# Expert weights fetched two slots at a time, and two narrow projections turned round, in a two-block model of one core

## The reference

```python
# block 1: one wide projection; 16 of its columns are the decay and beta inputs of the gated delta rule
(na_q, na_k, na_v, dn_qkv, dn_a, dn_b, dn_gate, df_q, df_k, df_v, ft_u) = split_proj(h_lat @ w_in)
g = -exp(a_log) * softplus(dn_a + dt_bias); beta = sigmoid(dn_b)
...
# block 1: 16 experts of width 2048, each takes the 32 tokens that score it highest
hid = silu(xg @ w_gate) * (xg @ w_up)
y = (hid @ w_down) * gate
```

## Time and profile before

| | |
|---|---|
| runs | 2237.03, 2241.74, 2240.36 us; median 2240.36 us |
| the profiled execution | 2242.1 us, of which the profile's span is 2240.3 us |
| PE busy | 1891.1 us (84%), 11984 instructions |
| DVE, ACT, POOL busy | 569.8, 279.6, 100.5 us |
| transfers | 728.94 MB, 102755 packets, mean 325 GB/s |
| granted PE clock, mean | 0.87 |

### The profile page before, as it was taken

How to read it: one execution, slowest core, us unless ns; L and a number is a source line. 1 busy time by engine, 2 the same in 40 slices (tenths; PEclk the granted TensorE clock), 3 DMA queues, 4 the chain that set the end, 5 groups by cost and what they waited for, 6 DMA issues and landing times.

```text
span 2240.3 us, 30046 instructions
## 1 busy us (share of the span) xinstructions
PE 1891.1 (84%) x11984; PEld 1017.9 (45%) x11984; DVE 569.8 (25%) x1180; ACT 279.6 (12%) x571; POOL 100.5 (4%) x131
## 2 busy tenths in 40 slices
PE   6999998877776777777766777899899899999998
PEld 3767777732222222222222222688788644444443
DVE  3774474430000000000000000342531422211222
ACT  3123331010000000000000000211530200000001
POOL 0002221000000000000000000100200000000000
PEclk9999999887777676777687777799999999999999
DMA  9542436199999999999999999334336989999997
GB/s 396 195 169 92 164 124 237 62 420 390 422 422 422 421 423 422 422 422 422 422 422 422 422 422 422 113 132 136 132 132 240 367 359 421 422 422 422 421 422 295
DMA packets 102755, 728.94 MB, mean 325 GB/s; under 512 B 11440, under 2 KB 11920, under 8 KB 16144
## 3 DMA queue, kind: packets, MB, share of 16 engines
q1 hardware_dynamic: 100368, 719.53, 79.0%
q10 hardware_dynamic: 2304, 8.24, 1.0%
HBM read 726.62 MB, written 1.10 MB: 325 GB/s over the span
## 4 chain that ended last, share of the span: by engine, by line
PE 61%; DMA 31%; DVE 4%; issue 2%; ACT 1%; POOL 1%; DVEq 0%; SPq 0%; ACTq 0%; PEldq 0%; POOLq 0%
DMA ring<-in_w_down 19%; PE psum L797 10%; DMA ring<-in_w_gate 10%; PE psum L934 7%; PE psum L829 5%; PE psum L530 4%; PE psum L1311 4%; PE psum L808 3%; PE psum L766 2%; PE psum L545 2%; PE psum L572 2%; DMA ring<-in_w_mod 2%; PE psum L1062 2%; PE psum L1212 1%; PE psum L1300 1%
## 5 line engine op out<-in xcount | busy, mean ns | idle before, releaser
L545 PE MATMUL psum<-ring,main 128*32 128x512 f32 x2016 | 308.3, 744 | 102.2 <-DMA ring<-in_w_up 49.8
L563 PE MATMUL psum<-ring,main 128*32 128x512 f32 x1016 | 189.1, 858 | 93.9 <-DMA ring<-in_w_down 83.4
L797 PE MATMUL psum<-ring,main 128*64 128x512 f32 x1024 | 225.9, 594 | 0.0
L545 PEld LDWEIGHTS psum<-ring,main 128*32 128x32 f32 x2016 | 59.4, 124 | 332.2 <-issue 118.5
L934 PE MATMUL psum<-main,ring 128*128 128x256 f32 x768 | 169.9, 381 | 0.0
L934 PEld LDWEIGHTS psum<-main,ring 128*128 128x128 f32 x768 | 146.3, 191 | 22.1 <-issue 0.5
L605 DVE TENSOR_TENSOR main<-main,psum 128x512 f32<-128x512 f32 x16 | 11.0, 688 | 522.4 <-ACT main L623 522.4
L797 PEld LDWEIGHTS psum<-ring,main 128*64 128x64 f32 x1024 | 73.2, 137 | 147.7 <-issue 147.7
L563 PEld LDWEIGHTS psum<-ring,main 128*32 128x32 f32 x1016 | 28.9, 133 | 235.9 <-DMA ring<-in_w_down 199.5
L530 PE MATMUL psum<-main 128*128 128x32 f32 x512 | 87.7, 342 | 26.3 <-DVE main L595 26.2
L829 PE MATMUL psum<-ring,main 128*64 128x512 f32 x480 | 106.3, 595 | 0.9 <-ACT main L903 0.9
(11 more groups left out here) (464 smaller groups left out, 2066.9 us busy)
## 6 DMA issues: line engine op xcount, KB each, us to landing
ring<-in_moe_w SPq DMA_DIRECT2D x188, 1024.0 KB, 15.7
ring<-in_w_down SPq DMA_DIRECT2D x127, 1024.0 KB, 25.9
...
```

The source lines that it names most:

```text
L545: last = mm(psum[32 * j:32 * j + 32, b, :], xg1[:, k, :], w[:, 512 * j:512 * j + 512], start=k == 0, stop=k == KT - 1)
L563: last = mm(psum[q:q + 32, BANK_Y, :], hidT[:, P * (f % 4) + 32 * (f // 4):P * (f % 4) + 32 * (f // 4) + 32], w[:, r, 512 * g:512 * g + 51 ...
L797: last = nc.tensor.matmul(psum[CAP2 * u:CAP2 * u + CAP2, b, :], xg2[:, 4 * h + k, CAP2 * u:CAP2 * u + CAP2], w[u][:, k, :], start=h == 0 a ...
```

## The change

**Expert transfers.** The weights of block 1's experts lie in one tensor, `w_moe1`, whose rows join gate and up of one slice (or four slices of down) to 16 KB; those of block 2 in `w_moe2`, whose rows join the two experts of a pair. One transfer now fills two neighbouring slots (`two_slots`), 2 MiB with 16 KB rows, is issued when both chunks before it have been used, and counts on the semaphore of the even slot. The chunks in spare places and one more (chunk 17 of expert 0) stay single, as 8 KB halves of such rows.

**Narrow projections.** Decay and beta: the weights, padded from 16 to 32 columns, are the stationary operand, four slices of the width in the four column groups, and the 512 tokens move (8 matmuls). ACT copies the four partial sums to `ab_part`, and after na_q four matmuls with `sum_experts` (a table of ones that adds the four groups) turn and add them into the tile `ab_sum`, from which DVE copies. `wi`: the same with 256 moving tokens (8 matmuls, `wi_part`), and two matmuls that add, placed after the first two tiles of scores. `IDXB` now alternates even and odd heads, and PE issues the matmuls of an even and an odd tile in turn. Two more PSUM tiles are handed out there, and one more in block 1.

**Kept.** The modulation sums on VectorE are as before.

The diff, cut to its core:

```diff
-                loads = [v + E1 * 24 // SLOTS - (s < SPARE1) for s, v in enumerate(loads)]
+                first1 = [v + 1 + (s >= SPARE1 and (s % 2 == 0 or s == SPARE1)) for s, v in enumerate(loads)]
+                loads = [v + 2 * (E1 - 1) * (s % 2 == 0) for s, v in enumerate(first1)]
...
-        w_ab = take(KT * 16).rearrange("p (k n) -> p k n", k=KT)
+        w_ab = take(KT * 32).rearrange("p (k n) -> p k n", k=KT)
...
+        ab_part = mpart[:, 0, :]
...
-            first = isinstance(e, int) and e == 0
-            fewer = 0 if first or s >= SPARE1 else 16
-            pe.wait_ge(loaded[s], 32 * e + 16 * (base1[s] + n // SLOTS + 1) - fewer)
+            if isinstance(e, int) and e == 0:
+                both = s - s % 2 if n > SLOTS + SPARE1 else s
+                pe.wait_ge(loaded[both], 16 * (base1[both] + n // SLOTS + 1))
+            else:
+                both = s - s % 2
+                pe.wait_ge(loaded[both], 32 * e + 16 * (first1[both] - 2 + n // SLOTS + 1))
...
-            name, c = (("w_gate", "w_up")[n % 2], n // 2) if n < 16 else ("w_down", n - 16)
-            src = A[name][8 * e + c] if isinstance(e, int) else \
-                A[name][bass.ds(8 * e + c, 1), :, :].rearrange("e p n -> p (e n)")
+            src = A["w_moe1"][12 * e + n // 2][:, WORDS * (n % 2):WORDS * (n % 2) + WORDS]
...
+
+        def two_slots(s):
+            return ring[:, s * WORDS:(s + 2) * WORDS]
+
+        def moe1_load_two(sp, e, m):
+
+            s = 2 * m % SLOTS
+            src = A["w_moe1"][12 * e + m] if isinstance(e, int) else \
+                A["w_moe1"][bass.ds(12 * e + m, 1), :, :].rearrange("e p n -> p (e n)")
+            sp.dma_start(two_slots(s), src).then_inc(loaded[s], 16)
...
+        wi_part = chosen[:, 0:S]
...
-        IDXB = [(t, par, pr) for t in range(NT) for par in range(2) for pr in range(2)]
+        IDXB = [(t, par, pr) for t in range(NT) for pr in range(2) for par in range(2)]
...
-            pe.wait_ge(loaded[n], 16 * j + 16 * (base2[n] + (n < 12 - SPARE2)))
+            both = n - n % 2
+            pe.wait_ge(loaded[both], 16 * j + 16 * (base2[both] + (n < 12 - SPARE2)))
...
+                src = A["w_moe2"][6 * i + n // 2][:, WORDS * (n % 2):WORDS * (n % 2) + WORDS]
...
             else:
-                sp.dma_start(slot(n), src).then_inc(loaded[n], 16)
+                src = A["w_moe2"][6 * i + n // 2] if isinstance(i, int) else \
+                    A["w_moe2"][bass.ds(6 * i + n // 2, 1), :, :].rearrange("e p n -> p (e n)")
...
-            w = chunk(("w_ki", 0))[:, 0:KT * (2 * IDD + IH)].rearrange("p (k n) -> p k n", k=KT)
+            w = chunk(("w_ki", 0))[:, 0:KT * (2 * IDD + 32)].rearrange("p (k n) -> p k n", k=KT)
             o = banks.new("ki")
             pe.wait_ge(*banks.free("ki"))
             for k in range(KT):
-                mm(o[:, 0:S], w[:, k, 0:P], uT[:, k, :], start=k == 0, stop=k == KT - 1)
-            for t in range(NT):
-                for k in range(KT):
-                    last = mm(o[:, S + IH * t:S + IH * t + IH], uT[:, k, P * t:P * t + P], w[:, k, P:P + IH], start=k == 0, stop=k == KT - 1)
+                last = mm(o[:, 0:S], w[:, k, 0:P], uT[:, k, :], start=k == 0, stop=k == KT - 1)
             last.then_inc(banks.when_full("ki"), 1)
-            last_user[("w_ki", 0)] = "ki"
+            o = banks.new("wi_part")
+            pe.wait_ge(*banks.free("wi_part"))
+            for turn in range(2):
+                for j in range(4):
+                    last = mm(o[32 * j:32 * j + 32, 0:S], w[:, 4 * turn + j, P:P + 32], uT[:, 4 * turn + j, :], start=turn == 0, stop=turn == 1)
+            last.then_inc(banks.when_full("wi_part"), 1)
+            last_user[("w_ki", 0)] = "wi_part"
 
             for ci in (1, 2):
                 pe.wait_ge(*banks.read_out(("in2", ci)))
             pe.wait_ge(*banks.read_out("ki"))
-            for t, par, pr in IDXB:
-                o = banks.new(("idx", t, par, pr))
-                pe.wait_ge(*banks.free(("idx", t, par, pr)))
-                for m in range(2):
-                    h = 4 * pr + 2 * m + par
-                    last = mm(o[:, S * m:S * m + S], qi[hpart(h), h // 2, P * t:P * t + P], ki[hpart(h), :], start=True, stop=True)
-                last.then_inc(banks.when_full(("idx", t, par, pr)), 1)
+            for t in range(NT):
+                for pr in range(2):
+                    for par in range(2):
+                        banks.new(("idx", t, par, pr))
+                        pe.wait_ge(*banks.free(("idx", t, par, pr)))
+                    for m in range(2):
+                        for par in range(2):
+                            h = 4 * pr + 2 * m + par
+                            last = mm(banks.tile(("idx", t, par, pr))[:, S * m:S * m + S], qi[hpart(h), h // 2, P * t:P * t + P],
+                                      ki[hpart(h), :], start=True, stop=True)
+                            if m == 1:
+                                last.then_inc(banks.when_full(("idx", t, par, pr)), 1)
+                    if t == 0 and pr == 0:
+                        o = banks.new("wi")
+                        pe.wait_ge(*banks.free("wi"))
+                        pe.wait_ge(*banks.read_out("wi_part"))
+                        for u in range(NT):
+                            last = mm(o[:, IH * u:IH * u + IH], wi_part[:, P * u:P * u + P], K("sum_experts")[:, 0:IH], start=True, stop=True)
+                        last.then_inc(banks.when_full("wi"), 1)
...
+                    for k2 in range(2):
+                        for j in range(4):
+                            last = mm(o[32 * j:32 * j + 32, :], w_ab[:, 4 * k2 + j, :], h3[:, 4 * k2 + j, :], start=k2 == 0, stop=k2 == 1)
+                    last.then_inc(banks.when_full("ab"), 1)
+                if name == "na_q":
+                    o = banks.new("ab_sum")
+                    pe.wait_ge(*banks.free("ab_sum"))
+                    pe.wait_ge(consts_loaded, 16)
+                    pe.wait_ge(*banks.read_out("ab"))
                     for t in range(4):
-                        for k in range(KT):
-                            last = mm(o[:, 16 * t:16 * t + 16], h3[:, k, P * t:P * t + P], w_ab[:, k, :], start=k == 0, stop=k == KT - 1)
-                    last.then_inc(banks.when_full("ab"), 1)
+                        last = mm(o[:, 16 * t:16 * t + 16], ab_part[:, P * t:P * t + P], K("sum_experts"), start=True, stop=True)
+                    last.then_inc(banks.when_full("ab_sum"), 1)
...
-            for n in range(SPARE1):
-                sp.wait_ge(m_chunk_used, n + 1)
-                moe1_load(sp, 1, n)
-            for n in range(SLOTS + SPARE1, 24):
-                sp.wait_ge(m_chunk_used, n - SLOTS + 1)
-                moe1_load(sp, 0, n)
-            for n in range(SPARE1, 24):
-                sp.wait_ge(m_chunk_used, 24 + (n - SLOTS + 1))
-                moe1_load(sp, 1, n)
+            for m in range(SPARE1 // 2):
+                sp.wait_ge(m_chunk_used, 2 * m + 2)
+                moe1_load_two(sp, 1, m)
+            sp.wait_ge(m_chunk_used, SPARE1 + 1)
+            moe1_load(sp, 0, SLOTS + SPARE1)
+            for m in range((SLOTS + SPARE1 + 1) // 2, 12):
+                sp.wait_ge(m_chunk_used, 2 * m + 2 - SLOTS)
+                moe1_load_two(sp, 0, m)
+            for m in range(SPARE1 // 2, 12):
+                sp.wait_ge(m_chunk_used, 24 + 2 * m + 2 - SLOTS)
+                moe1_load_two(sp, 1, m)
             with sp.Fori(2, E1) as e:
-                for n in range(24):
-                    sp.wait_ge(m_chunk_used, 24 * e + (n - SLOTS + 1))
-                    moe1_load(sp, e, n)
+                for m in range(12):
+                    sp.wait_ge(m_chunk_used, 24 * e + (2 * m + 2 - SLOTS))
+                    moe1_load_two(sp, e, m)
...
-            for n in (4, 5):
-                moe2_load(sp, 0, n)
+            moe2_load(sp, 0, 4)
...
-            for n in range(12 - SPARE2, 12):
+            for n in range(12 - SPARE2, 12, 2):
                 moe2_load(sp, 1, n)
-            for n in (0, 1, 2, 3, 6, 7):
-                sp.wait_ge(*banks.full(last_user[holder2[n]] if n < FRONT else ("wo2", 1, 1)))
+            for n in (0, 2, 6):
+                if n < FRONT:
+                    sp.wait_ge(*banks.full(last_user[holder2[n]]))
+                    sp.wait_ge(*banks.full(last_user[holder2[n + 1]]))
+                else:
+                    sp.wait_ge(*banks.full(("wo2", 1, 1)))
                 moe2_load(sp, 0, n)
-            for n in range(12 - SPARE2):
-                sp.wait_ge(n_chunk_used, n + 1)
+            for n in range(0, 12 - SPARE2, 2):
+                sp.wait_ge(n_chunk_used, n + 2)
                 moe2_load(sp, 1, n)
             with sp.Fori(2, PAIRS2) as i:
-                for n in range(12):
-                    sp.wait_ge(n_chunk_used, 12 * i + (n - 11))
+                for n in range(0, 12, 2):
+                    sp.wait_ge(n_chunk_used, 12 * i + (n - 10))
```

(28 more changed lines are left out.)

20 lines of the change are left out of this document (6 added, 14 removed).

## The result

The changed kernel takes 2217.65 us (median of 4 runs, 2215.49 to 2223.9), beside 2241.05 for the kernel before on the same chip: a ratio of 0.9899, 95% interval 0.9869 to 0.9929. Measured again later (E9): 2218.82 beside 2239.9, 0.9913, 0.9893 to 0.9933. The prediction was 2233.9 with a range of 2222 to 2241. The sign was right, the size was not: rival 2, larger rows are faster (chance 0.20), came true. The profiled execution took 2219.53 us, its span is 2217.8.

A forecast was written before the change was run, and what follows sets the result against it. The transfer stream was taken to bound block 1's experts, and PE block 2's experts and most of the mixers. Pace 0, gap 0, end +1.9, decay and beta -2.4, indexer -6.0 gave -6.5 from 2240.36: 2233.9 us, range 2222 to 2241.

The forecast's parts named there:

- rival 2: Expert transfers: larger rows are faster, by 0.6% to 1.5% of 912 us; run at 2219 to 2228; chance 0.20.
- The pace: Block 1's expert stream, 367 chunks in 912 us: no change from larger rows, 0, bounds 4.3 us either way.
- the doubled bound: Pace of the expert stream: twice the 4.3 us allowed on either side for the range.
- The gaps: Stream between block 1's experts: cost 0 in steady state; behind expert 0 also 0, bounds -1 and +1 us.
- The end: Block 1's last expert chunks: PE finds two landed together, not one, +1.9 us, between 1.1 and 2.0.
- Decay and beta: Block 1's projections: 3.1 us gained, less 0.7 for half clock, so -2.4 us, bounds -3.5 and 0.
- half clock behind the longer wait: Block 1, PE's transposes after waiting for VectorE: half clock lasts longer, costing 0.7 us, range 0 to 1.5.
- rival 4: Small gains swallowed: block 1's half clock takes all 2.4, the indexer keeps 2.7 of 6; 2239.6 us; chance 0.15.
- The indexer: Block 2's `wi` and score tiles: earlier start and overlapping heads gain 6 us, between 2.7 and 7.3.
- the bank of the second tile: Indexer: transposes behind the score tiles need this bank, free at about 1448.9, so PE can't go on before 1449.
- The sum: Whole kernel: 0 (pace) + 0 (gap) + 1.9 (end) - 2.4 - 6.0 = -6.5 us, giving 2233.9 us.

The follow-up runs named there:

- E9: Changed kernel plus 22 unread matmuls in PE's wait of 10.46 us in block 1: 2218.31 us, then 2214.66 beside the changed kernel's 2218.82.
- E2: Kernel before with rows of 4 KB in block 1's experts, transfers still 1 MiB: 2265.28 us.
- E7: Kernel before with chunk 4 of expert 1 asked for behind expert 0's last chunk: 2239.63 us, beside 2239.32 for the kernel before.
- E8: Kernel before with half the change: first kernel, new transfers alone, 2223.43 us (0.9936); second kernel, new projections alone, 2233.04 us (0.9978).
- E10: Changed kernel with 22 unread matmuls in block 1's wait and eleven or so more in PE's waits from 400 to 440 us: 2213.84 us (0.9881).

## Why the prediction was wrong, step by step

**The pace: the step that failed.** The prediction priced larger rows at 0, with 4.3 us either way, and left 0.20 to rival 2. Measured, 1 MiB takes 2.485 us in packets of 8 KB and 2.447 in packets of 16 KB: 367 chunks by 0.038 are 14.0 us, outside even the doubled bound. All sizes lie on one line, within 0.001 us:

| row | packets for 1 MiB | us for 1 MiB | 2.409 + 0.000594 x packets |
|---|---|---|---|
| 4 KB | 256 | 61.44 / 24 = 2.560 | 2.561 |
| 8 KB | 128 | 59.65 / 24 = 2.485 | 2.485 |
| 16 KB | 64 | 58.73 / 24 = 2.447 | 2.447 |
| 24 KB | 42.7 | 7.30 / 3 = 2.434 | 2.434 |
| 32 KB | 32 | 9.71 / 4 = 2.428 | 2.428 |

Spread over 16 engines, a packet costs 9.5 ns on its engine beside the time of its bytes, and the line ends at 1,048,576 B / 2.409 us = 435 GB/s. The packet records of the traces agree: from 600 to 1300 us a packet of 8 KB takes 313.6 ns on average and one of 16 KB 614.7, so twice the bytes take 12.5 ns less than twice the time; the records of neighbours overlap by some 3 ns. Each packet here is one row in memory, so whether the cost belongs to the packet or to the start of a row no run tells. The Trainium skill has both parts ("DMA: Bandwidth & Descriptors"): the ceiling, 435 GB/s in the section "Where 436 GB/s comes from", agrees; the cost of a packet in "Why small descriptors are slow (HBM only)", 3 cycles, is 3.5 ns at the 850 MHz of the first, an estimate from that page, and the runs show 2.7 times that.
What misled was a window with a second queue in it. The earlier trace rows has 5 us with 616 packets and 5 us with 291, both with 2.12 MB. Without the completion writes these are 551 and 259 packets, and by 9.5 ns a packet the first window should be 0.17 us, 3.5%, slower. It is not, in any number of executions: in the 17 traces of this record, alike at this place, the first window has 422.5 GB/s on average (415 to 426) and the next 423.5 (419 to 429). The view of the kernel before tells the queues apart, first in the one window, then in the next:

```profile
q1 hardware_dynamic: 474, 2.06, 100.2%
q10 hardware_dynamic: 142, 0.06, 4.4%
...
q1 hardware_dynamic: 291, 2.12, 101.7%
```

SP's queue, where 350 of the 474 packets are of 4 KB, moves 411 GB/s in the first window (409 on average of the 17 traces), which is the rate of rows of 4 KB in E2, 410. The small packets of the other queue came on top of it: the packet times of both add up to 104.6% of the window, where one queue alone has 101.7%. So the cost per packet was in these rows, and the second queue's bytes filled it up; that the two queues overlap in this way is read from the rows, and no run tried it. The steady stream has one queue and no such filling. The prediction also leant on a window of which it said that it can't tell less than 1% apart.

**The gaps.** Cost 0 in the steady state was right: 58.73 us for each expert from the fourth on. The third takes 59.25 (558.05 to 617.30), so half a microsecond is lost once there. For the gap behind expert 0 the prediction had 0, within 1 us: single profiles scatter by 3 us, but on average the stream gained 13.8 us where the pace gives 14.0 (E7), so 0 was right.

**The end.** Predicted +1.9, measured +0.3: the last pair did take 3.50 us instead of 1.98, but the spreading behind it ran at full clock.

**Decay and beta.** The mechanism was right, and the times within 0.3 us: PE at df_k's end at 116.16 (116.1), VectorE's copy at 81.74 (81.5), the wait of 3.63 us gone, the transposes 2.94 us earlier (3.1), no half clock between 77 and 85. The term behind it was mis-sized: half clock behind the longer wait was put at 0.7 us, 1.5 at most, and took 3.3, from 2.9 ahead at 158.49 to 0.4 behind at 176.67. E9 shows that it was the clock. So 2.4 of gain became 0, the end of its bounds, as rival 4 had it for this half.

**The indexer.** Right in size, in part by luck. The projection behind the tiles comes 7.1 us nearer to `ki` (6 forecast, 7.3 at most), and 5.9 of them reach block 2's experts. In this execution PE found the clock at 0.57 from 1698 to 1702 us, behind a wait of 1.96 us, and its 64 matmuls there took 15.74 us for 14.05; in E8's second kernel and in E10 they took 14.05. The tiles start 1.0 us behind `ki` (1.3), and half clock is gone. PE goes on 8.96 us behind `ki`'s start, where the prediction had the bank of the second tile hold it until 8.9. But ScalarE had read that bank by 1431.75 us, 8.1 behind, and PE's row at 1432.57 has no wait: what set the time was the tiles' own 4.0 us.

**The sum.** -14.0 (pace) - 5.9 (indexer) + 0.3 (end) + 0.3 (front) are -19.3, as much as E8's two halves bring (-19.6); the 3.0 more of the profile lie in the stream and are scatter (E7), and so may be what the medians have more, -21 and -23. The prediction's own -6.5 with rival 2's 1.5% of 912 us, 13.7, gives -20.2, so 2220.2 against the 2217.65 measured: the pace is the term on which it went wrong.
